# Sparse-attention value products of one Trainium2 kernel: one 128-column weight set for four heads, or two 64-column sets for even and odd heads

## What is computed

```python
o_c = jnp.einsum('bqkgc,bckd->bqkgd', p_c, v_cmp)        # 15 compressed blocks
o_s = jnp.einsum('bqkgnj,bqknjd->bqkgd', p_s, v_sel)     # selected blocks
o_w = jnp.einsum('bqkgw,bwkd->bqkgd', p_w, vwb)          # window
o = gb[..., 0:1] * o_c + gb[..., 1:2] * o_s + gb[..., 2:3] * o_w
...
return out @ w_out
```

## Time and profile before

| | us |
|---|---|
| median of 3 runs (720.53 to 723.85) | 723.19 |
| the profiled execution, its own time | 723.07 |
| its span in the profile | 721.3 |
| PE / DVE / ACT busy in the span | 670.7 / 490.5 / 394.9 |
| attention of layer 0 from its first scores to the end of the last window | 78.3 to 174.8 |

### The profile page before, as it was taken

How to read it: one execution, slowest core, us unless ns; L and a number is a source line. 1 busy time by engine, 2 the same in 40 slices (tenths; PEclk the granted TensorE clock), 3 DMA queues, 4 the chain that set the end, 5 groups by cost and what they waited for, 6 DMA issues and landing times.

```text
span 721.3 us, 11799 instructions
## 1 busy us (share of the span) xinstructions
PE 670.7 (93%) x4196; PEld 583.9 (81%) x4196; DVE 490.5 (68%) x922; ACT 394.9 (55%) x767; POOL 33.7 (5%) x61
## 2 busy tenths in 40 slices
PE   5999896999989999999999999787989999999995
PEld 4998565666889999999997788655889999999994
DVE  4387469684587777766678555685687777766675
ACT  5454334663585555555556455363685555555554
POOL 0200034000000000000000100302000000000000
PEclk9999998999999999999999999989999999999998
DMA  7465053000626544445541554420536545555521
GB/s 265 159 212 182 27 206 116 2 1 1 217 107 241 196 176 175 175 178 191 202 187 59 192 175 169 165 88 1 203 121 240 187 181 179 175 177 186 200 79 58
DMA packets 19614, 109.10 MB, mean 151 GB/s; under 512 B 2432, under 2 KB 2816, under 8 KB 10240
## 3 DMA queue, kind: packets, MB, share of 16 engines
q1 hardware_dynamic: 19584, 108.71, 41.9%
HBM read 107.65 MB, written 1.05 MB: 151 GB/s over the span
## 4 chain that ended last, share of the span: by engine, by line
PE 78%; DVE 12%; ACT 5%; DMA 2%; issue 2%; POOL 1%; SPq 0%; POOLq 0%; DVEq 0%; ACTq 0%
PE psA L356 11%; PE psA L357 11%; PE psA L358 11%; PE psT L452 6%; PE psO L454 6%; PE psO L453 6%; PE psO L452 6%; PE psT L454 6%; PE psT L453 6%; PE psO L641 2%; PE psO L617 2%; DVE stat L1461 2%; DMA stage<-in_w_group 2%; DVE win_lo L1227 2%; DVE arena L1495 1%
## 5 line engine op out<-in xcount | busy, mean ns | idle before, releaser
L1308 DVE TENSOR_TENSOR win_lo<-stage,win_hi 128x1024 fp32r<-128x1024 f32 x90 | 109.4, 1219 | 5.7 <-ACT win_hi L926 5.7
L1324 DVE SCALAR_TENSOR_TENSOR arena<-psO,prm,arena 128x255 f32<-128x255 f32 x84 | 40.1, 478 | 90.8 <-ACT arena L944 90.8
L926 ACT ACTIVATE win_hi<-stage 128x1024 fp32r<-128x1024 f32 x92 | 96.0, 1050 | 6.4 <-PE psA L358 6.4
L452 PE MATMUL psT<-hA_hi,win_hi 128*128 128x256 f32 x336 | 95.2, 283 | 1.7 <-DVE hA_lo L1243 1.7
L453 PE MATMUL psO<-hA_lo,win_hi 128*128 128x256 f32 x336 | 95.2, 283 | 0.0
L452 PE MATMUL psO<-hA_hi,win_hi 128*128 128x256 f32 x336 | 95.2, 283 | 0.0
L454 PE MATMUL psT<-hA_hi,win_lo 128*128 128x256 f32 x336 | 95.2, 283 | 0.0
L454 PE MATMUL psO<-hA_hi,win_lo 128*128 128x256 f32 x336 | 95.2, 283 | 0.0
L453 PE MATMUL psT<-hA_lo,win_hi 128*128 128x256 f32 x336 | 95.2, 283 | 0.0
L1227 DVE TENSOR_TENSOR win_lo<-stage,win_hi 128x1024 fp32r<-128x1024 f32 (+3 forms) x56 | 62.3, 1152 | 32.2 <-ACT win_hi L874 31.9
L944 ACT ACTIVATE arena<-psO,prm 128x256 f32<-128x256 f32 x42 | 23.7, 563 | 89.7 <-PE psO L454 89.7
(11 more groups left out here) (242 smaller groups left out, 1358.9 us busy)
## 6 DMA issues: line engine op xcount, KB each, us to landing
stage<-in_w_ffn_in SPq DMA_DIRECT2D x44, 1024.0 KB, 5.4
stage_out<-in_w_ffn_out SPq DMA_DIRECT2D x44, 516.0 KB, 3.5
stage<-in_w_kv SPq DMA_DIRECT2D x8, 1024.0 KB, 4.8
stage<-in_w_group SPq DMA_DIRECT2D x5, 1024.0 KB, 5.1
stage<-in_w_phi SPq DMA_DIRECT2D x4, 1024.0 KB, 4.9
stage<-in_w_nsa_out SPq DMA_DIRECT2D x4, 1024.0 KB, 5.0
stage<-in_w_dq SPq DMA_DIRECT2D x4, 1024.0 KB, 4.8
stage<-in_w_dout SPq DMA_DIRECT2D x4, 1024.0 KB, 4.8
```

The costliest lines, as they stand in the source:

```text
L452: mm(o, win_hi[:, slot, cs], hA_hi[:, k, :], start=k == 0, stop=False)
L926: act.activation(win_hi[:, slot, h * W // 2:(h + 1) * W // 2], stage[:, slot, h * W // 2:(h + 1) * W // 2], ACT.Copy).then_inc(sem["in_hi" ...
L1308: last = dve.tensor_tensor(win_lo[:, slot, cs], stage[:, slot, cs], win_hi[:, slot, cs].bitcast(F32), sub)
L1324: dve.scalar_tensor_tensor(conv[:, b, g, k:S], (psT, psO)[g][:, b, 0:S - k], prm[:, b, 4 * g + 2 - k:4 * g + 3 - k], conv[:, b, g, k:S], A ...
```

## The change

1. `vals` holds each value head once: 512 columns in place of 1024. The two evictions (L1448, L1055) write 128x512 in place of 128x1024.
2. `nsa_pv` uses 64 weight columns. Each matmul of 512 moving columns becomes two of 256: the even heads of the group (moving data with a step of two heads) write PSUM partitions 0 to 63, the odd heads 64 to 127, in turn. The four compressed matmuls keep 128 moving columns and also go by turns to the two halves.
3. The bank of a window so has its result in columns 0 to 255 of all 128 partitions. `oT_hi` and `oT_lo` are one 128x256 instruction each in place of two of 64x256; each counts its semaphore by two, so the other waits stay as they are, but DVE waits for the whole of `oT_hi`.
4. The compressed values are made once: L674 has 64 moving columns in place of 128, and each of the eight evictions (L1122) writes 128x128 elements in place of 128x256.

```diff
--- before.py
+++ after.py
@@ -179,11 +179,11 @@
         hid_b = tokA_flat[:, 1024:1536].rearrange("p (v f) -> p v f", v=2)[0:64]
         hidT = tokA_flat[:, 1536:1664].rearrange("p (t c) -> p t c", t=2)
         hidTv = arena[:, 3072:4096].rearrange("p (t g r c) -> p t g r c", t=2, g=KVH, r=8)
-        vcmp = tokB_flat.rearrange("p (h d) -> p h d", h=HEADS)
+        vcmp = tokB_flat[:, 0:HEADS * HD].rearrange("p (h d) -> p h d", h=HEADS)
         xs = tokB_flat.rearrange("p (t c) -> p t c", t=TT)
         o_tok = tokB_flat.rearrange("p (t h d) -> p t h d", t=TT, h=DH)
         final_g = tokA_flat[:, 0:D]
-        vals_nsa = vals[:, :, :].rearrange("p t (y g u d) -> p t y g u d", y=2, g=KVH, u=2)
+        vals_nsa = vals[:, :, 0:2 * KV_W].rearrange("p t (y g d) -> p t y g d", y=2, g=KVH)
 
 
         ssq = stat[:, 0:TT]
@@ -614,11 +614,14 @@
                         pe_.wait_ge(sem["oT_lo"], 2 * (w - 1))
                 o = psO[:, w % 2, :]
                 for b in range(nb):
-                    mm(o, vals_nsa[:, b, y, g, :, :].rearrange("p u d -> p (u d)"),
-                       pT[:, w % 2, y * nb + b, :, :].rearrange("p h q -> p (h q)"), start=y == 0 and b == 0, stop=False)
+                    for e in range(2):
+                        mm(o[e * 64:e * 64 + 64, 0:S].rearrange("p (m q) -> p m q", m=2), vals_nsa[:, b, y, g, :],
+                           pT[:, w % 2, y * nb + b, e:GROUP:2, :], start=y == 0 and b == 0, stop=False)
                 if y == 1:
                     for j in range(GROUP):
-                        last = mm(o[:, j * P:(j + 1) * P], vcmp[:, 4 * g + j, :], cmp_pT[:, t, g // 2, :], start=False, stop=j == GROUP - 1)
+                        m, e = j // 2, j % 2
+                        last = mm(o[e * 64:e * 64 + 64, m * P:(m + 1) * P], vcmp[:, 4 * g + j, :], cmp_pT[:, t, g // 2, :],
+                                  start=False, stop=m == 1)
                     last.then_inc(sem["oT_bank"], 1)
 
             def cmp_scores(t):
@@ -671,9 +674,9 @@
             pe_.wait_ge(sem["cmp_masked"], 8)
             for g in range(KVH):
                 for c in range(2):
-                    last = mm(psO[:, 1, g * P:(g + 1) * P],
+                    last = mm(psO[:, 1, g * HD:(g + 1) * HD],
                               hidTv[:, c, g, :, :].rearrange("p r c -> p (r c)"),
-                              w2[:, 1, c, :], start=c == 0, stop=c == 1)
+                              w2[:, 1, c, 0:HD], start=c == 0, stop=c == 1)
             last.then_inc(sem["vcmp_bank"], 1)
             nsa_pv(0, 0)
             for u in range(4, len(UNITS)):
@@ -1052,9 +1055,7 @@
                                    ACT.Copy).then_inc(sem["kT_act"], 1)
 
             act.wait_ge(sem["in_used"], N_A)
-            act.activation(vals_nsa[:, 1, :, :, :, :].rearrange("p y g u d -> p (y g) u d"),
-                           psA[:, 3, :].rearrange("p (h d) -> p h d", d=HD).unsqueeze(2).to_broadcast([P, 8, 2, HD]),
-                           ACT.Copy, scale=rstd[:, 1:2]).then_inc(sem["proj_act"], 1)
+            act.activation(vals_nsa[:, 1, :, :, :].rearrange("p y g d -> p (y g d)"), psA[:, 3, :], ACT.Copy, scale=rstd[:, 1:2]).then_inc(sem["proj_act"], 1)
             def exps(u, t, pre, waits_free):
 
                 nk = (t + 1) * P
@@ -1085,10 +1086,8 @@
             def oT_hi(w):
                 g, t = w // TT, w % TT
                 act.wait_ge(sem["oT_bank"], w + 1)
-                for e in range(2):
-                    act.activation(hB_hi[e * 64:e * 64 + 64, 2 * g:2 * g + 2, t * P:(t + 1) * P],
-                                   psO[e * 64:e * 64 + 64, w % 2, :].rearrange("p (m e q) -> p e m q", m=2, e=2)[:, e],
-                                   ACT.Copy).then_inc(sem["oT_hi"], 1)
+                act.activation(hB_hi[:, 2 * g:2 * g + 2, t * P:(t + 1) * P], psO[:, w % 2, 0:S].rearrange("p (m q) -> p m q", m=2),
+                               ACT.Copy).then_inc(sem["oT_hi"], 2)
 
             exps(0, 0, "", free_nsa)
             exps(1, 0, "", free_nsa)
@@ -1119,7 +1118,7 @@
 
             act.wait_ge(sem["params_in"], 16)
             for r in range(8):
-                act.activation(vcmp[:, r:HEADS:8, :], psO[:, 1, :].rearrange("p (g d) -> p g d", g=KVH)[:, r // 4:KVH:2], ACT.Copy,
+                act.activation(vcmp[:, r:HEADS:8, :], psO[:, 1, 0:KVH * HD].rearrange("p (g d) -> p g d", g=KVH)[:, r // 4:KVH:2], ACT.Copy,
                                scale=rowmask[:, r:r + 1]).then_inc(sem["vcmp_ready"], 1)
             act.wait_ge(sem["cmpT_bank"], 1)
             act.activation(cmp_pT.rearrange("p t b q -> p (t b q)"), psO[:, 1, :], ACT.Copy).then_inc(sem["cmpT_ready"], 1)
@@ -1445,9 +1444,7 @@
 
             dve.wait_ge(sem["in_used"], N_A)
             dve.wait_ge(sem["rstd"], 1)
-            dve.tensor_scalar(vals_nsa[:, 0, :, :, :, :].rearrange("p y g u d -> p (y g) u d"),
-                              psA[:, 2, :].rearrange("p (h d) -> p h d", d=HD).unsqueeze(2).to_broadcast([P, 8, 2, HD]),
-                              rstd[:, 0:1], None, ALU.mult).then_inc(sem["proj_dve"], 1)
+            dve.tensor_scalar(vals_nsa[:, 0, :, :, :].rearrange("p y g d -> p (y g d)"), psA[:, 2, :], rstd[:, 0:1], None, ALU.mult).then_inc(sem["proj_dve"], 1)
 
             lam_in = cols[:, O_LAM:O_COS].rearrange("p (a b d) -> p a b d", a=2, b=2)
             dve.tensor_tensor(rope_t[:, 0, :, 0:4, :].rearrange("p a h r -> p a (h r)"), lam_in[:, :, 0, :], lam_in[:, :, 1, :], ALU.mult).then_inc(sem["lam_prod"], 1)
@@ -1471,12 +1468,9 @@
             NU = KVH * TT * 2
             def oT_lo(w):
                 g, t = w // TT, w % TT
-                for e in range(2):
-                    dve.wait_ge(sem["oT_hi"], 2 * w + e + 1)
-                    dst = slice(e * 64, e * 64 + 64)
-                    dve.tensor_tensor(hB_lo[dst, 2 * g:2 * g + 2, t * P:(t + 1) * P],
-                                      psO[dst, w % 2, :].rearrange("p (m e q) -> p e m q", m=2, e=2)[:, e],
-                                      hB_hi[dst, 2 * g:2 * g + 2, t * P:(t + 1) * P].bitcast(F32), sub).then_inc(sem["oT_lo"], 1)
+                dve.wait_ge(sem["oT_hi"], 2 * w + 2)
+                dve.tensor_tensor(hB_lo[:, 2 * g:2 * g + 2, t * P:(t + 1) * P], psO[:, w % 2, 0:S].rearrange("p (m q) -> p m q", m=2),
+                                  hB_hi[:, 2 * g:2 * g + 2, t * P:(t + 1) * P].bitcast(F32), sub).then_inc(sem["oT_lo"], 2)
 
 
             dve.wait_ge(sem["gates_ready"], 1)
```

## The result

The changed kernel takes **713.57 us** in the median (712.77 to 713.82, 4 runs), the kernel before 723.09 beside it (720.53 to 723.85, 4 runs): ratio 0.9873, interval 0.9859 to 0.9888, so 1.3% faster. The prediction said 716.2 in a range of 714.0 to 723.4. The profiled execution took 713.82 us, with a span of 712.0 (before: 723.07 and 721.3).

A forecast was written before the change was run, and what follows sets the result against it. In a group, PE was taken to bound some 11.8 us and DVE 3.1. Savings of 0.5 (values), 0.7 (compressed), 1.7, 1.4, 0.8 and 1.9 us (attention stretches) made 7.0 off 723.07: 716.1, median 716.2, range 714.0 to 723.4.

The forecast's parts named there:

- n calls (2n instructions) take n+1 steps: Value products on PE: column halves overlap like the scores' row halves, 0.215 us a step for 256 columns; 9.0 us together.
- change of array shape: Products behind transposes: 13 new switches between whole array and 128*64, 0.1 us each, +1.3 us; ends 0 and 0.2.
- t = 0, two calls: Value products at L617: two calls of 256 columns take 0.64 in place of 0.86 us, -0.22, 8 times.
- t = 1, four calls: Value products at L617: four calls take 1.06 in place of 1.72 us, -0.66, 8 times.
- L621, four calls of 128 columns: Compressed value products: eight instructions of 128 columns take 0.65 in place of 0.89 us, -0.24, 8 times.
- The overlap of the three queues: Layout of units 4 to 15: PE's part of a group falls 1.84 us, waits for DVE return 0.4, saving 1.4.
- The evictions: Each window's result: single evictions save ACT 0.39 us, off the path, and DVE 0.43 us a window, 8 times.
- The values, "in full", and the compressed values: Ahead of the loop: L1448's shorter eviction saves 0.53 us in full; eight shorter L1122 evictions save 0.7 us before L689.
- rival C: PE's new idle time lowers the clock; one fall of some 5 us costs 2.5, 718.7 us; 0.07 with partly cut overlap.
- the clock at 1.00 from 122 us on: Sign expected in the changed trace: PE's granted clock stays at the full level from 122 us on.
- Rival A: Value products: column halves do not overlap, products keep 1.72 and 0.86 us; 723.0 us, no change; chance 0.14.
- Rival B: Even-to-odd turns at L617 and L621: 80 exposed weight loads of 137 ns, 11 us, no overlap; 732.3 us; chance 0.09.

The follow-up runs named there:

- Experiment 1: The changed kernel with each window's result evicted in two 64x256 instructions on ACT and two on DVE, as before; 714.77 us.
- experiment 8: The changed kernel with the unused products of experiment 6, but 8 in place of 32 before the transposes of unit 3; 707.71 us.
- experiment 9: Experiment 8 with values and compressed values written twice again; 709.57 us.
- experiment 3: The changed kernel with values and compressed values written twice again, the products reading the first copy; 713.91 us.
- experiment 2: The changed kernel with even and odd heads on the same column half, evicted in two pieces, DVE waiting for both of ACT's; 722.81 us.
- Experiment 4: The changed kernel with all calls of the even heads in a window first, then all of the odd heads; 712.92 us.
- experiment 6: The changed kernel with unused products in PE's waits: 6, 11 and 32 in the first attention, 26 and 6 in the second; 709.68 us.
- experiment 10: The kernel before with all the unused products of experiment 8; 718.63 us.

## Why the prediction was wrong in its size and right in its mechanism

**The step that failed** is "n calls (2n instructions) take n+1 steps". It read the scores' 1.06 us for eight instructions as five steps of 0.215. Narrow looks at the same scores, before the change, show four pairs:

```profile
141.86 0.49 PE L586 MATMUL psA<-keysT,qrT 64*128 64x256 f32 x2
...
142.39 0.38 PE L586 MATMUL psA<-keysT,qrT 64*128 64x256 f32 x2
...
142.61 0.38 PE L586 MATMUL psA<-keysT,qrT 64*128 64x256 f32 x2
```

The second pair starts at 142.18 and the masks at 142.92. So the distances are 0.32, 0.21, 0.22 and 0.31: four steps of 0.215, and 0.1 twice, once behind the first pair and once in front of the masks. The second 0.1 is the change of array shape, which the prediction knew at 0.09 us; that the first is a weight load that nothing hides is a guess. A distance that ends at another shape was divided as if it held columns alone, and the rows to see this were in the trace before the change. The changed kernel shows what n calls take where the shape stays:

| term | forecast | measured | 8 times, forecast | measured |
|---|---|---|---|---|
| t = 0, two calls | 0.86 to 0.64 | 0.86 to 0.48 | -1.8 | -3.0 |
| t = 1, four calls | 1.72 to 1.06 | 1.72 to 0.91 | -5.3 | -6.5 |
| L621, four calls of 128 columns | 0.89 to 0.65 | 0.89 to 0.44 | -1.9 | -3.6 |

Together 13.1 us of PE in place of 9.0. With the change of shape at 0.1, 13 times, as taken (0.09 measured), PE's work falls by 11.8 where 7.7 was forecast. Of this the loop passes on 8.66 (forecast 5.8).

**The overlap of the three queues** came out as laid out: 5.8 of 7.7 us of PE's saving were to reach the end of the loop, and 8.66 of 11.8 did, three quarters both times. That DVE would take part of the saving back came true, and more of it: a group's PE work falls by 2.88 us (2 x 0.38 + 2 x 0.81 + 2 x 0.45 - 4 x 0.1), the group by 1.99, so 0.9 us is given back where 0.4 was forecast. DVE is busy 11.74 of 12.90 us, and it is nearly the bound of the group now.

**The evictions**: lengths as forecast. Experiment 1 gives 1.17 us of the loop for them, 0.15 us a window; the prediction had put DVE's share at what it keeps of PE's saving, without a figure of its own.

**The values, "in full", and the compressed values**: the 0.53 us came at the scores of unit 1, where the prediction had it, and in every profile: 2.40 or 2.41 us behind unit 0 with the values once, 2.93 or 2.94 with them twice. The compressed values were to give 0.7; experiments 8 and 9, with the clock at 1.00 at this place in both, give 0.95 there. Both terms were right as work. Whether they arrive as time is not shown for the kernel as it is: experiment 3 finds 0.3 us by the medians and 1.3 by the profiles. The prediction carried the clock as rival C inside the loop only, where it stayed at 1.00 (window above). It fell ahead of the loop, in both kernels, and its sign "the clock at 1.00 from 122 us on" failed: it was at 0.50 until past 126 us. The trace of before had it in its rows: 117 to 119 us at 0.50. In the profiled pair the clock gives the changed kernel 1.6 us at the second attention's output projection, which is luck, and the start takes 1.0 back; how much of the 9.5 us of the medians is luck is not shown.

**Rival A** (the halves don't overlap, 723.0) is what experiment 2 built but for the evictions, and its 722.81 is near that price; the change itself is not it. **Rival B** (the other half's weight load exposed) would have made eight instructions over 2 us; they take 0.91. The Trainium skill (TensorE: Matmul & The Clock Gate, The mechanism) says that a weight load overlaps products in flight only where the row groups differ. Here both halves have the same 128 rows, and the 0.91 us disagree with it: beside the four steps there is 0.05 us, too little for one load of 137 ns. The same section has it that matmuls start in the order of the program. Experiment 4's even calls all stand ahead of the odd ones. If one half does one pass at a time, as in experiment 2, and no odd one starts ahead of the last even one, eight instructions take at least seven steps, 1.5 us; they take 0.92, so the two disagree, unless the order was changed before it came to PE. The records don't tell even from odd, so which started first is not shown.

**The range** left 714.0 as its lower end; the only better case that the prediction priced was a change of shape at no cost (714.9). The bound on the other side of the overlap, n steps in place of n+1, was not priced; it is worth 4.1 us of PE's work, and 2.9 us of the loop.

## What to carry to other kernels

Where products with 64 columns of weights come in twos, send their results to the two halves of the array's columns: n calls then take the time of n/2, and evicting the full bank at once follows from it. Before dividing a distance between starts by a step, look at the starts one by one, or use a run whose end has the same shape. Where the clock falls near a saving, don't read the saving from one pair of profiles: look first at how far the profiles of one program lie apart there (2.5 us here). 57 unused products in PE's waits took off 5.2 to 5.9 us, more than half of what the change did.

## What was not expected of the hardware

- Instructions of the two column halves run as pairs, two in 0.44 us, the pairs 0.22 to 0.26 us apart, and they do so when the program has both calls of one half first (experiment 4).
- How much the clock costs around short waits. With 6, 11 and 32 unused products at three places the phi products took 7.05 us where 8.61 were seen, and the scores behind unit 3's transposes 1.13 where it was 2.08; all changes of experiment 8 together are worth 5.2 to 5.9 us. Too many cost: 32 in place of 8 is 2.0 us by the medians (experiments 6 and 8). Too few don't hold it each time: with 8, the clock was at 1.00 behind them in the profiles of experiments 8 and 9 and at 0.50 in that of experiment 10.
- Short DVE instructions were slow while POOL worked on the window of weights. Timeline after, 98 to 118 us, then experiment 8:

```profile
104.97 4.66 POOL L839 TENSOR_TENSOR win_lo<-stage,win_hi 128x1024 fp32r<-128x1024 f32 x2
105.26 2.08 DVE L1461 TENSOR_SCALAR stat<-stat 128x4 f32<-128x4 f32 x1
```

```profile
110.06 4.67 POOL L851 TENSOR_TENSOR win_lo<-stage,win_hi 128x1024 fp32r<-128x1024 f32 x2
114.78 1.14 DVE L1501 TENSOR_SCALAR arena<-arena,stat 128x256 f32<-128x256 f32 x4
```

L1461 on 128x4 takes 0.17 us in the loop, where POOL has nothing to do, and 2.08 us here. The four scalings of 128x256 (L1501, in the changed kernel L1489) take 1.14 us in experiment 8, where they start just behind POOL's end, and 5.27 us in the changed kernel, where they start 0.09 us behind POOL's start (111.85 and 111.76). It is so in both kernels; taking POOL's work away was not tried.
